# A two-layer decoder trunk on one core: where the norm's sums and root stand at the passages between stages

## The reference

```python
def rms_norm(x, g, eps=NORM_EPS):
    y = xf * lax.rsqrt(jnp.mean(xf * xf, axis=-1, keepdims=True) + eps)
    return (y * g.astype(jnp.float32)).astype(x.dtype)
def sq_relu_mlp(x, w_in, w_out):
    return jnp.square(jax.nn.relu(x @ w_in)) @ w_out
...
    for layer in range(DEPTH):
        hn = rms_norm(h, norm_mix_pre[layer])
        m = mixer_ab(hn, ...) if layer % 2 == 0 else mixer_ret(hn, ...)
        h = h + rms_norm(m, norm_mix_post[layer])
        f = sq_relu_mlp(rms_norm(h, norm_ffn_pre[layer]), ffn_w_in[layer], ffn_w_out[layer])
        h = h + rms_norm(f, norm_ffn_post[layer])
```

## Time and profile before

| | |
|---|---|
| device time, three runs | 1477.74, 1478.39, 1479.36 us (median 1478.39) |
| span of the profiled execution (first to last instruction) | 1476.8 us |
| busy in it: PE, PEld, DVE, ACT, POOL | 97%, 80%, 62%, 36%, 6% |
| chain that ended last | PE 89%, DVE 6%, ACT 2%, issue 1%, DMA 1%, POOL 1% |
| mean granted clock of the PE | 0.983 of full speed |

### The profile page before, as it was taken

The page is one execution under the profiler, slowest core; times in us unless marked ns, Lnnn a source line. Parts: engine busy times, 40 slices in busy tenths (PEclk is TensorE's granted clock), DMA queues, the critical chain, the costliest instruction groups (busy, mean ns, idle before and its releaser), DMA issues.

```text
span 1476.8 us, 22066 instructions
## 1 busy us (share of the span) xinstructions
PE 1436.1 (97%) x9650; PEld 1183.2 (80%) x9650; DVE 921.3 (62%) x1200; ACT 538.7 (36%) x632; POOL 87.2 (6%) x89
## 2 busy tenths in 40 slices
PE   9999999998999999998999999999998999999997
PEld 6778777776888888887888888888887788888786
DVE  7768676667655565554665445355447776868654
ACT  7455454533312221223343332332434433433322
POOL 0000000012010100001200000000003000000000
PEclk9999999998999999999899999999998999999999
DMA  5211111101573644631212222222130352434332
GB/s 187 73 36 59 50 59 45 59 30 35 209 270 141 229 175 175 235 110 62 86 58 88 83 86 86 83 89 86 58 114 29 123 191 86 171 115 165 134 112 59
DMA packets 30623, 160.21 MB, mean 108 GB/s; under 512 B 2816, under 2 KB 6912, under 8 KB 15552
## 3 DMA queue, kind: packets, MB, share of 16 engines
q1 hardware_dynamic: 23456, 130.73, 24.4%
q0 software_dynamic: 7072, 28.08, 5.1%
HBM read 144.12 MB, written 14.68 MB: 108 GB/s over the span
## 4 chain that ended last, share of the span: by engine, by line
PE 89%; DVE 6%; ACT 2%; issue 1%; DMA 1%; POOL 1%; DVEq 0%; POOLq 0%
PE bank L388 20%; PE bank L394 20%; PE bank L391 20%; PE bank L691 2%; PE bank L694 2%; PE bank L695 2%; PE bank L1684 2%; PE bank L1681 2%; PE bank L1678 2%; PE bank L996 2%; PE bank L402 1%; PE bank L1003 1%; DVE WL L346 1%; PE bank L593 1%; PE bank L589 1%
## 5 line engine op out<-in xcount | busy, mean ns | idle before, releaser
L388 PE MATMUL bank<-XH,WH 128*128 128x512 f32 x944 | 379.2, 402 | 16.1 <-DVE XL L481 12.6
L394 PE MATMUL bank<-XH,WL 128*128 128x512 f32 x944 | 371.6, 394 | 0.0
L391 PE MATMUL bank<-XL,WH 128*128 128x512 f32 x944 | 371.6, 394 | 0.0
L346 DVE TENSOR_TENSOR WL<-raw,WH 128x2048 fp32r<-128x2048 f32 (+1 forms) x99 | 222.2, 2246 | 148.1 <-ACT WH L340 148.1
L340 ACT ACTIVATE WH<-raw 128x2048 fp32r<-128x2048 f32 (+1 forms) x99 | 185.3, 1873 | 195.5 <-DMA raw<-weights 195.3
L388 PEld LDWEIGHTS bank<-XH,WH 128*128 128x128 f32 x944 | 179.8, 190 | 60.3 <-issue 20.8
L394 PEld LDWEIGHTS bank<-XH,WL 128*128 128x128 f32 x944 | 179.6, 190 | 38.7
L391 PEld LDWEIGHTS bank<-XL,WH 128*128 128x128 f32 x944 | 179.7, 190 | 38.0 <-issue 1.9
L847 ACT ACTIVATE AH<-relu 128x512 fp32r<-128x512 f32 (+1 forms) x64 | 37.9, 592 | 209.1 <-DVE relu L876 209.1
L388 PE MATMUL bank<-AH,WH 128*128 128x512 f32 x256 | 99.7, 389 | 0.0
L394 PE MATMUL bank<-AH,WL 128*128 128x512 f32 x256 | 99.6, 389 | 0.0
(11 more groups left out here) (360 smaller groups left out, 2339.8 us busy)
## 6 DMA issues: line engine op xcount, KB each, us to landing
raw<-weights SPq DMA_DIRECT2D x104, 1024.0 KB, 4.8
block<-weights POOLq DMA_DIRECT2D x12, 1024.0 KB, 5.5
sums_of_blocks<-block POOLq DMA_DIRECT2D x12, 1024.0 KB, 5.4
raw<-sums_of_blocks SPq DMA_DIRECT2D x12, 1024.0 KB, 4.8
raw<-weights SPq DMA_DIRECT2D x8, 512.0 KB, 4.8
h<-x_fm SPq DMA_DIRECT2D x4, 512.0 KB, 7.9
out_tm<-h SPq DMA_DIRECT2D x8, 256.0 KB, 2.6
rc<-ret_const POOLq DMA_DIRECT2D x1, 1536.0 KB, 7.4
```

The costliest lines, as they stand in the source:

```text
L346: nc.vector.tensor_tensor(WL[i][:, :n], raw[i][:, :n], WH[i][:, :n], ALU.subtract).then_inc(S("w_lo"), 1)
L388: mm = pe.matmul(bank[b][:], wh, xh, start=(k == 0), stop=False)
L391: mm = pe.matmul(bank[b][:], wh, xl, start=False, stop=False)
L394: mm = pe.matmul(bank[b][:], wl, xh, start=False, stop=(k == len(xs) - 1))
```

## The change

**What it does.** In the three passages the sums stand behind all eight kt of the first four tiles, and the spread of the root further behind. In the FFN the fifth and sixth output tiles go to banks 6 and 7, the seventh and eighth to 0 and 1; the spread stands between the fifth and the sixth tile. Chunk 3 is split after tile 0 instead of tile 2, in ACT and in DVE. In the retention v of chunk 2 is computed by pairs of token tiles: first tokens 0 and 1 (banks 2, 3) over its four kt, with the spread in the middle, then, after the wait for rb_ready, tokens 2 and 3 (banks 4, 5). Chunk 3 of the retention is split ahead of the turning of q and not between q and k. No instruction is added or taken away.

```diff
         def quarter_at(c0, layer, q):
             return FFN1_AT[q] if layer else c0 + 8 * q
+        FIRST_BANKS = (0, 1, 2, 3, 6, 7, 0, 1)
+        def ffn_bank(q, j):
+            return FIRST_BANKS[j] if q == 0 and j < 8 else j % 4
+        def split_after(q, j):
+            return {0: 3, 4: 4, 6: 5}.get(j) if q == 0 and j < 8 else j // 2 + 2 if j % 2 == 0 else None
...
-                        units(pe, use, range(4), ws, X, 1, ready, (0, 6))
+                        units(pe, use, range(4), ws, X, 1, ready)
                         pre_sums_pe(pe, m)
-                        units(pe, use, range(4), ws, X, 0, ready, (6, 7))
-                        pre_spread_pe(pe, m)
-                        units(pe, use, range(4), ws, X, 0, ready, (7, 8))
...
-                        units(pe, use, [(j + k) % 4], [columns(cj, k)], X if j < 8 else A, left,
+                        units(pe, use, [ffn_bank(q, j + k)], [columns(cj, k)], X if j < 8 else A, left,
                               a_tile if j == 8 and k == 0 else None)
+                        if q == 0 and j == 4 and k == 0:
+                            pre_spread_pe(pe, m)
...
-                    if j % 2 == 0 and (q or j):
-                        split_lo(dve, c + j // 2 + 2)
+                    if split_after(q, j):
+                        split_lo(dve, c + split_after(q, j))
...
+                    ahead = hd == 0 and half == 0
+                    for k, ts in [(k, ts) for ts in ((0, 1), (2, 3)) for k in range(4)] if ahead else [(k, range(TT)) for k in range(4)]:
+                        if ahead and (k, ts) == (2, (0, 1)):
+                            pre_spread_pe(pe, m)
+                        if ahead and (k, ts) == (0, (2, 3)):
+                            pe.wait_ge(S("rb_ready"), m + 1)
+                        for t in ts:
...
-                if hd:
-                    split_lo(dve, c + 2)
+                split_lo(dve, c + 2 if hd else c + 3)
...
                         qk_low(0)
-                        split_lo(dve, c + 3)
+                        if hd:
+                            split_lo(dve, c + 3)
```

More of the change, by code:

```diff
@@ L840, in ffn_act @@
                 for j in range(8 if layer else 16):
-                    b = j % 4
+                    b = ffn_bank(q, j)
                     if layer and q < SEVEN and j > 4:
@@ L851, in ffn_act @@
                         use.next(b)
-                    if j % 2 == 0 and (q or j):
-                        split_hi(act, c + j // 2 + 2)
+                    if split_after(q, j):
+                        split_hi(act, c + split_after(q, j))
                     if layer and q == 1 and j in (1, 3):
@@ L1652, in ret_pe @@
                     ready = x_tiles(pe, m)
-                    units(pe, use, [0, 1, 6, 7], cols, X, 1, ready, (0, 6))
+                    units(pe, use, [0, 1, 6, 7], cols, X, 1, ready)
                     pre_sums_pe(pe, m)
-                    units(pe, use, [0, 1, 6, 7], cols, X, 0, ready, (6, 7))
-                    pre_spread_pe(pe, m)
-                    units(pe, use, [0, 1, 6, 7], cols, X, 0, ready, (7, 8))
-                    pe.wait_ge(S("rb_ready"), m + 1)
                 else:
@@ L1672, in ret_pe @@
                     chunk_ready(pe, cv)
-                    for k in range(4):
+                    ahead = hd == 0 and half == 0
+                    for k, ts in [(k, ts) for ts in ((0, 1), (2, 3)) for k in range(4)] if ahead else [(k, range(TT)) for k in range(4)]:
                         kt = half * 4 + k
                         wh, wl = (w[cv % RING][:, k * T:(k + 1) * T] for w in (WH, WL))
-                        for t in range(TT):
+                        if ahead and (k, ts) == (2, (0, 1)):
[3 more added lines that the diff above has]
+                        for t in ts:
                             tok = slice(t * P, (t + 1) * P)
@@ L1763, in ret_act @@
                     use.next(b)
-                if hd:
-                    split_hi(act, c + 2)
+                split_hi(act, c + 2 if hd else c + 3)
                 for i in range(2):
@@ L1769, in ret_act @@
                         nc.scalar.activation(qkH[here][i][:, k, :], qk[here][i][:, k, :], ACT.Copy).then_inc(S("qk_hi"), 1)
-                    if i == 0:
+                    if i == 0 and hd:
                         split_hi(act, c + 3)
```

## The result

The change makes the kernel slower: 1487.02 us (median of 4 runs, 1485.63 to 1489.13) against 1478.07 (4 runs, 1476.19 to 1479.36) of the kernel before beside it. The ratio is 1.0064, 95% interval 1.0050 to 1.0079, or 7.4 to 11.7 us. Predicted were 1485.3 and a range of 1480 to 1491.

A forecast was written before the change was run, and what follows sets the result against it. The PE, busy for 97% of the span, was taken to bound the kernel, so only its idle or slow time counts. A +4.4, B -3.2 and C +5.7 gave +6.9 on 1478.4, or 1485.3 us, range 1480 to 1491.

The forecast's parts named there:

- the late root: FFN passages: the spread behind the fifth tile delays rB and DVE's first relu, 6.0 us later in A.
- A, +4.4: First FFN passage: DVE's eighth AL comes at 397.45 instead of 393.07, the PE has no slack, 4.4 us lost.
- some 5 us in all: Passage A, sign in the new profile: the PE's waits for relu and AL.
- C, +5.7: Last FFN passage: DVE's fourth relu and so chunk 5 come 5.7 us later, and the PE waits for it.
- B, -3.2: Retention passage: v starts earlier, a wait for chunk 4 takes 0.9 us, 3.2 us gained.
- v starts 4.6 us earlier: Passage B: without wait and slow clock at the sums, v starts at 726.2 instead of 730.80.
- rival 3: All passages: the clock falls behind the sums even without idle time, 1.6 us each, 1490.1; chance 0.12.
- Rival 1: A and C: DVE absorbs the late root, the kernel is faster, 1472.0; chance 0.07.
- Rival 2: Only C pays; A has slack at the eighth AL and is -2.1, sum 1478.8; chance 0.12 with its weaker form.
- Its weaker form: The two idle banks of A and C are worth nothing, B alone counts, 1475.2; chance 0.12 together with rival 2.

The follow-up runs named there:

- root_later: The change with the FFN's spread of the root one tile later, behind the sixth tile: 1504.89 us, ratio 1.0185 to the kernel before.
- early_third: The change with the FFN's spread behind the fifth tile's second kt and chunk 3 split after the third tile as before: 1478.89 us, ratio 1.0008 to before.
- banks_only: The kernel before with only the change's order of banks for the FFN's output tiles: 1478.28 us, ratio 1.0001.
- ffn_only: The kernel before with the change's FFN edits alone (passages A and C), the retention as before: 1489.53 us, ratio 1.0090.
- ninth_bank2: The change with the first quarter's ninth to sixteenth units in banks 2, 3, 0, 1 and so on: 1497.44 us, one run.
- ret_only: The kernel before with the change's retention edits alone (passage B), both FFN as before: 1478.34 us, ratio 1.0013.
- before_again: The unchanged kernel before, executed and profiled a second time: 1478.30 us, ratio 1.0006.
- one_kt_ffn: The kernel before with sums one kt later and spread three matmuls behind bank 0's kt 7, in A and C alone: 1474.73 us, ratio 0.9980.
- one_kt_later: The kernel before with sums one kt later and spread three matmuls behind the first bank's kt 7, in all three passages: 1474.80 us, ratio 0.9980.
- one_kt_ret: The kernel before with sums one kt later and spread three matmuls behind the first bank's kt 7, in B alone: 1477.25 us, ratio 1.0001.
- root_early: The change with the FFN's spread behind the fifth tile's second kt, not behind the tile: 1484.71 us, ratio 1.0055 to the kernel before.

## Why the prediction was right, point by point

**The time** was right (1485.3 against 1487.02), the sign too, and the cause: the late root (root_later, early_third). Of its three terms two hold in their mechanism, with sizes somewhat off, and one failed. The times of the terms are taken here as means over the profiles in which a passage is unchanged (five each) and those in which it is as in the change.

**A, +4.4: right, somewhat small.** Unchanged 362.5, 363.0, 361.8, 361.4 and 364.4, mean 362.6 (the last is banks_only, whose banks are those of the change). As in the change (after, ffn_only) 368.3 and 368.4: +5.7, within its bounds of +3.3 to +6.2. The steps: fifth tile 25.04 us after the entry (362.98), predicted 364.05 - 338.77 = 25.28. First relu at 31.89, predicted 32.08. Eighth AL at 58.48, predicted 58.68. The PE's start on it was predicted at that same moment and came 0.95 later. This is the step that fell short: I had let the wait for bank 0 (some 3 us; 3.11) and the slow matmuls behind it disappear into the wait for the AL. There were 14 such matmuls, and they outlasted it. The upper bound held 8 of them, 0.2 each. Of the waits told beforehand, "some 5 us in all", 3.9 came: 0.75 for chunk 3 and 3.11 for the bank.

**C, +5.7: the right mechanism, somewhat large.** Unchanged 353.9, 355.2, 354.7, 353.7 and 355.3, mean 354.5; as in the change (after, ffn_only, ninth_bank2) 358.3, 360.9 and 359.2, mean 359.5: +4.9. Its lower bound was +5.3. The second product waits for 6.52 us, in ffn_only 6.53, in ninth_bank2 6.52, where some 7 were predicted. In the profile after, the second product comes 5.11 later: the fifth tile was predicted 1148.63 - 1122.92 = 25.71 us after the entry and starts after 25.07, since 7 matmuls were slow at this entry and 10 at the one that the prediction was read from. What comes back in the third quarter (0.9 us) makes most of the rest; I had looked for no such slack.

**B, -3.2: wrong.** Unchanged 421.6, 418.4, 418.3, 419.6 and 420.7, mean 419.7. With the retention's edits 420.2, 420.0, 420.7, 420.1, 421.0, 420.8 and 419.8, mean 420.4: no gain, if anything a loss, as ret_only says by its time. The step that failed is "v starts 4.6 us earlier". In the profile after it does so by 4.25. But the 29.50 of before were those of one execution, with 12 slow matmuls behind the sums. In the other four unchanged passages v starts 26.6 to 27.9 after the entry, and in the seven changed ones 25.3 to 26.4. The head start is some 2 us, and the wait for chunk 4 takes most of it: the gate starts 48.4 to 51.3 after the entry in the unchanged (mean 49.5) and 49.2 to 50.5 in the changed (mean 49.8). That wait was priced at 0.9, and is 1.42 in the change and 1.17 to 1.71 in the other six: the DMA of chunk 3 lands 5.46 us after v starts (predicted 5.05), and DVE waits 0.46 more inside k. The two unchanged passages without a fall behind the sums (before_again and one_kt_ffn, 418.4 and 418.3) are even 2 us shorter than the changed ones: the edits seem to take the fall away and give back as much, though two profiles are few.

The means add up to +11.3; the measured ratio allows 7.4 to 11.7, and the sum said +6.9. A was too low by 1.3 and B by 3.9, and only C, too high by 0.8, stands against them. That the time came within 1.7 us of the forecast is so in part luck: the measured difference of 9.0 lies below what the means of the terms add up to. The means are of two to seven profiles each and carry a scatter of their own.

**The clock.** The claim that it stays up behind sums without an idle time before them held in all 27 passages with later sums and in the seven unchanged ones without one, so rival 3 is refuted. What removing the falls is worth I had read from one profile: 12 slow matmuls of B, 8 of A. Over the five unchanged executions of each passage the mean is 5.4 in A, 5.4 in B and 3.0 in C (from the table above), at some 0.2 us each 1.1, 1.1 and 0.6 us. one_kt_later, which removes them all and little else, gains 3.0 (0.9 to 5.0 by its interval), which agrees with their sum of 2.8. one_kt_ffn alone gains 3.0 too (1.6 to 4.3), where A and C give 1.7 by this count. The Trainium skill (TensorE: Matmul & The Clock Gate, "What's actually happening") says that the number of matmuls at the lower clock differs between runs of one kernel. I had cited it as untested. There the Trainium skill speaks of a kernel's start; in two profiles of this kernel the same holds at later places (6 and 12 slow matmuls at the entry of B, 12 and 0 behind its sums).

**The other rivals.** Rival 1, the root absorbed: refuted by the waits in A and C. Rival 2, only C pays: refuted by A. Its weaker form, the banks worth nothing by themselves, is true for the banks (banks_only, 1.0001), and no defence, since the change uses them to put work ahead of the root.

**What is open.** C in ffn_only is 2.6 us longer than in the change. 1.4 of that stand already at the start of its fifth tile (26.49 us after the entry against 25.07), with 14 slow matmuls at the entry against 7; the rest is open. So is the source of the gain of one_kt_ffn. Whether B has a part in the gain of one_kt_later isn't settled: one_kt_ret's interval, -1.9 to +2.2 us, holds both nothing and the 1.1 worked out above.

## What to carry to other kernels

Ahead of a value for which another engine waits with its whole chain, put only as much work as hides the wait. Between kt 5 and the spread stood 12 matmuls before; 15 were the fastest (0.998), 30 made no measurable difference with the old place of the split (early_third) and cost 8 us with the new one (root_early), 48 cost 9 us and 72 cost 27. Place a prefetched operand's split by when its data lands, and move it again when the chain around it moves. And before you price the removal of slow matmuls, look at a second profile of the same kernel: those of one profile may be absent in the next.

## What the runs showed of the hardware that was not expected

The number of slow matmuls behind the same idle time of 4.2 us varies from 6 to 14 over the 42 entries, whose code is the same up to there; in two executions of one program it is 6 and 12 at the entry of B. In the fifteen passages of the table it goes with whether the PE waits at the sums (0.05 to 0.57 us) and the clock falls again. In banks_only 7 slow matmuls followed a start of the sums only 0.44 us after the last matmul (0.23 is back to back), while 0.28 in ret_only had none.

Nor does the length of an idle time ahead of full-size matmuls tell here whether the clock falls. The second of the seven products in C waits 1.98 us for its weights in one_kt_later and in one_kt_ffn, whose code there is the same. The stretch behind this wait, first of one_kt_later, then of one_kt_ffn:

```profile
1174.22:1179.00 4.78, 4.78 (x14) 3.77 (x15) 4.57 (x9) 2.53 (x3) 0.00 (x0) 0.64 0.60 219
```
```profile
1174.04:1179.00 4.96, 4.96 (x22) 4.01 (x23) 4.75 (x9) 2.65 (x4) 0.00 (x0) 1.00 0.55 211
```

In early_third a wait of 3.18 us at the same place is followed by 1.00 too, while the 3.11 of the ninth unit in the change were followed by 0.56.

The first stage, which no kernel here changes, took 337.9 to 347.1 us. Where it was long (343.1 to 347.1, five profiles), one stretch of it had a lower clock, 0.73 or 0.80. That stretch in ffn_only (first stage 344.9) and before (338.8):

```profile
75.00:100.00 25.00, 23.18 (x426) 18.76 (x426) 10.64 (x18) 11.85 (x14) 0.00 (x0) 0.73 0.01 3
```
```profile
75.00:100.00 25.00, 23.33 (x461) 19.19 (x460) 12.69 (x22) 14.79 (x19) 0.00 (x0) 1.00 0.01 3
```

The PE is about as busy in both (23.18 and 23.33 us), with 426 matmuls against 461. This is why the spans of single profiles were never compared, only the stretches between entries. What brings the lower clock there was not looked into.
